# Token sums by columns, and a 31-tap convolution with an early shift, two taps on VectorE and another weight order

## The reference, cut to what matters

```python
def conv_module(h, ...):                       # first layer of the first block, for x and for ctx
    u = h @ w_pw1 + b_pw1                      # 1024 -> 2048
    a, gt = jnp.split(u, 2, axis=-1)
    u = a * jax.nn.sigmoid(gt)
    u = conv_general_dilated(u, w_dw, ...) + b_dw     # depthwise, 31 taps along the tokens
    u = jax.nn.silu(layernorm(u, ln_g, ln_b))  # mean and variance over the 1024 features
    return u @ w_pw2 + b_pw2
# every layer: mod = silu(c) @ w_mod + b_mod gives scales, shifts and gates;
#   h = rmsnorm(x, g) * (1 + sc) + sh ;  x = x + gate * rmsnorm(y, g)
#   second block: x = layer_norm(ALPHA * x + y, g, b), twice in each of two layers
```

## Time and profile before

| | us |
|---|---|
| three runs | 1966.68, 1968.42, 1971.39 |
| median | 1968.42 |
| span of the profiled execution | 1969.0 |
| TensorE busy | 1889.2 |
| VectorE, ScalarE, GpSimd busy | 1201.8, 953.6, 542.5 |

### The profile page before, as it was taken

One profiled execution on the slowest core, in us unless ns is written; L12 is line 12 of the kernel. 1 busy time (PEld: TensorE's weight loads), 2 busy tenths in 40 slices (PEclk: granted clock), 3 DMA queues, 4 the chain that ended last, 5 costly groups with the idle time before them and its releaser, 6 DMA issues.

```text
span 1969.0 us, 36121 instructions
## 1 busy us (share of the span) xinstructions
PE 1889.2 (96%) x14718; PEld 1668.6 (85%) x14718; DVE 1201.8 (61%) x2440; ACT 953.6 (48%) x1709; POOL 542.5 (28%) x685
## 2 busy tenths in 40 slices
PE   6999999999998989999998999999999999999998
PEld 4855778888886857899987989999999899989997
DVE  4989763233338575655579675685648876567473
ACT  4314532232224477544456474565555556456464
POOL 1320010000001533000021222747373322374736
PEclk9999999999999999899999999999999999999999
DMA  9335442222224254655544444455554544545551
GB/s 358 128 108 206 151 150 96 97 97 97 97 97 171 86 193 175 211 182 182 183 160 175 142 136 160 165 168 172 194 182 152 174 148 133 168 150 178 187 178 59
DMA packets 84548, 307.24 MB, mean 156 GB/s; under 512 B 9376, under 2 KB 10656, under 8 KB 84128
## 3 DMA queue, kind: packets, MB, share of 16 engines
q1 hardware_dynamic: 84384, 304.94, 45.4%
HBM read 303.86 MB, written 1.05 MB: 155 GB/s over the span
## 4 chain that ended last, share of the span: by engine, by line
PE 82%; DVE 10%; ACT 5%; DMA 2%; issue 1%; SPq 0%; POOL 0%; DVEq 0%; ACTq 0%
PE pb L540 18%; PE pb L542 18%; PE pb L541 18%; PE pb L513 7%; PE pb L514 6%; PE pb L519 6%; DVE wlo L1897 2%; DMA raw<-wstream 2%; ACT whi L1237 1%; PE pb L591 1%; DVE Y L2146 1%; PE pb L765 1%; PE pb L924 1%; PE pb L1108 1%; PE pb L1121 1%
## 5 line engine op out<-in xcount | busy, mean ns | idle before, releaser
L540 PE MATMUL pb<-Hh,whi 128*128 128x256 f32 (+1 forms) x2304 | 701.8, 305 | 1.8 <-DVE SM L2480 1.6
L542 PE MATMUL pb<-Hh,wlo 128*128 128x256 f32 (+1 forms) x2304 | 694.6, 301 | 0.0
L541 PE MATMUL pb<-Hl,whi 128*128 128x256 f32 (+1 forms) x2304 | 694.6, 301 | 0.0
L1237 ACT ACTIVATE whi<-raw 128x1024 fp32r<-128x1024 f32 x468 | 489.3, 1054 | 318.1 <-PE pb L542 171.2
L2855 POOL TENSOR_TENSOR wlo<-raw,whi 128x256 fp32r<-128x256 f32 x576 | 434.9, 790 | 734.9 <-ACT whi L1237 733.9
L1897 DVE TENSOR_TENSOR wlo<-raw,whi 128x1024 fp32r<-128x1024 f32 x324 | 421.2, 1305 | 344.1 <-ACT whi L1237 343.7
L540 PEld LDWEIGHTS pb<-Hh,whi 128*128 128x128 f32 x2304 | 441.9, 192 | 22.9 <-DVE SM L2480 2.5
L541 PEld LDWEIGHTS pb<-Hl,whi 128*128 128x128 f32 x2304 | 442.2, 192 | 15.0
L542 PEld LDWEIGHTS pb<-Hh,wlo 128*128 128x128 f32 x2304 | 442.0, 192 | 15.0
L513 PE MATMUL pb<-Hh,whi 128*128 128x256 f32 (+1 forms) x528 | 161.2, 327 | 4.6 <-ACT Hh L1311 3.2
L514 PE MATMUL pb<-Hh,wlo 128*128 128x256 f32 (+1 forms) x528 | 158.8, 322 | 0.0
(11 more groups left out here) (333 smaller groups left out, 2952.6 us busy)
## 6 DMA issues: line engine op xcount, KB each, us to landing
raw<-wstream SPq DMA_DIRECT2D x572, 512.0 KB, 3.5
X<-xin SPq DMA_DIRECT2D x2, 1024.0 KB, 7.7
out<-X SPq DMA_DIRECT2D x8, 128.0 KB, 1.8
CON<-consts SPq DMA_DIRECT2D x1, 926.0 KB, 8.6
VEC<-vecs SPq DMA_DIRECT2D x1, 662.0 KB, 9.5
CON<-consts SPq DMA_DIRECT2D x1, 147.0 KB, 3.8
VEC<-vecs SPq DMA_DIRECT2D x1, 88.0 KB, 2.0
```

What stands on the lines that cost most here:

```text
L540: e.matmul(dst, hi, xh, start=k == 0, stop=False)
L541: e.matmul(dst, hi, xl, start=False, stop=False)
L542: i = e.matmul(dst, lo, xh, start=False, stop=k == kt - 1)
L1237: e.activation(whi[:, s % NPIECE, :], raw[:, p % NRAW, :], ACT.Copy).then_inc(sig("act_hi", ("hi", p)), 1)
```

## The change

- **Statistics.** `quarters` and its copies become `columns`: for each 128 tokens one matmul with the data as the stationary operand (128 x 128) and one column of 1/1024 as the moving one. The result is one column for each 128 tokens, so a statistic is 128 x 4 (or 128 x 2). The small steps work on these, `widen` spreads a column with the identity as the moving operand (two matmuls instead of four for 256 tokens), and the constant `quad` is gone.
- **Shift.** The rough mean is summed before the first tap and spread after tap 3 (before: after taps 8 and 13); it is stored negative. The start of the taps waits for each tile of `U` in its turn.
- **Taps.** TensorE makes 29 taps. VectorE makes the last two of tiles 4 to 7 with the shift added, into four tiles `part` (`part_taps`), and 16 matmuls with `blocks` add these in; the 32nd "tap" is gone.
- **Moving out.** VectorE moves out results 4, 6 and 5, ScalarE 7; VectorE squares 5.
- **Stream.** The first four tiles of `w_pw2` stand ahead of C; C has three groups (12 pieces) and N three. Six halves of C run at taps 2, 5, 8, 11, 14 and 17, one of N at tap 26.
- **Split.** GpSimd makes no `wlo` for `w_pw1` any more; it makes those of the third and fourth piece of `w_pw2`, behind the last chunk of `DG`. VectorE makes the others.

```diff
-MODS = {"S0": (0, 2, 2), "S1": (1, 2, 2), "C": (4, 4, 1), "N": (8, 2, 1), "F": (10, 3, 1), "A": (13, 3, 1),
+MODS = {"S0": (0, 2, 2), "S1": (1, 2, 2), "C": (4, 3, 1), "N": (7, 3, 1), "F": (10, 3, 1), "A": (13, 3, 1),
...
-    mod("C")
-    run([("conv_w_pw2", (0,), m * 128) for m in range(8)], FIRST, then=["N"])
+    run([("conv_w_pw2", (0,), m * 128) for m in range(8)], FIRST, then=["C", "N"])
...
-            if tag == "pw1":
-                return s > 5 and s % 3 == 0
+            if s in (tile_turn["pw1", 15] + 3, tile_turn["pw1", 15] + 4):
+                return True
...
+            def columns(b, o, tile, n, start, stop, point):
+                for c in range(n // 128):
+                    i = e.matmul(b[:, o + c:o + c + 1], tile[:, c * 128:(c + 1) * 128], con("mean", 0, 1),
+                                 start=start and c == 0, stop=stop and c == n // 128 - 1)
+                i.then_inc(sig("pe_stat", point), 1)
...
-                for c in range(4):
-                    i = e.matmul(b[:, c * n // 4:(c + 1) * n // 4], con("quad", c, c + 1).broadcast_to((128, 128)), r,
+                for c in range(n // 128):
+                    i = e.matmul(b[:, c * 128:(c + 1) * 128], r[:, c:c + 1].broadcast_to((128, 128)), con("ident"),
                                  start=True, stop=True)
...
+            bank("norm", ("stat", "cs"), ("root", "cs"))
+            w.wait_ge(*on("cv", 0))
+            token_sums("cs", Y[:, 0:512], 512, True, False, ("zsum", "cs"))
+            w.wait_ge(*on("cv", 1))
+            token_sums("cs", Y[:, 512:1024], 512, False, True, ("sums", "cs"))
             w.wait_ge(*on("pad"))
-            for ct in range(4):
-                w.wait_ge(*on("u", 4 + ct))
-            for i_ in range(CONVW + 1):
+            for i_ in range(CONV_PE):
                 c, q = i_ // CHUNK, i_ % CHUNK
                 w.wait_ge(*on("dg", c))
                 dg = DG[:, c % 3, :, :, :]
                 for ct in range(4):
+                    if i_ == 0:
+                        w.wait_ge(*on("u", 4 + ct))
...
+                if i_ == 24:
+                    feed("N")
-                if i_ % 3 == 2 and i_ < 30:
+                if i_ % 3 == 2 and (i_ < 18 or i_ == 26):
                     bite(1)
+                if i_ == 23:
+                    mod_tr("mods")
-                if i_ == 13:
+                if i_ == 3:
                     w.wait_ge(*on("root", "cs"))
                     widen("cs", 512, ("shift",), ring="norm")
...
+            for ct in range(4):
+                w.wait_ge(*on("part", ct))
+                for r in range(4):
+                    rows = slice(32 * r, 32 * r + 32)
+                    i = e.matmul(got[r][32 * ct:32 * ct + 32, :], con("blocks", p0=32 * r, p1=32 * r + 32),
+                                 slots.at(("part", ct))[rows, :], start=False, stop=True)
...
+            def part_taps(ct):
+                t = buf(1.02, "part", ("part", ct), ("conv", 3))
+                w.wait_ge(*on("shift"))
+                w.wait_ge(*on("u", 4 + ct))
+                for i in range(CONV_PE, CONVW):
+                    if i > CONV_PE:
+                        w.wait_ge(*on("tap", 4 + ct, i - 1))
+                    points = [("tap", 4 + ct, i)] + ([("part", ct)] if i == CONVW - 1 else [])
+                    e.scalar_tensor_tensor(out=two(t), in0=U[:, 4 + ct, :, i:i + T], scalar=vec("conv_w_dw", i * 8 + 4 + ct),
+                                           in1=two(slots.at("shift") if i == CONV_PE else t), op0=ALU.mult, op1=ALU.add).then_inc(
+                        sig("dve_conv", *points), 1)
...
             shift(2)
             shift(3)
-            lo_to(("pw1", 15), 2)
+            for ct in range(4):
+                part_taps(ct)
             mod_add("C")
...
             for c, (i0, n) in enumerate(CHUNKS):
-                if c == 3:
-                    lo_to(("pw1", 15), 0)
                 for u in slots.take(0, "dg", ("dg", c), ("dgused", c)):
                     w.wait_ge(*u)
...
+            lo_to(("pw1", 15), 4)
```

More of the change, by code:

```diff
@@ L26 @@
 CONVW = 31
+CONV_PE = 29
 PAD = 15
@@ L29 @@
 CHUNK = 8
-CHUNKS = [(i, min(CHUNK, CONVW - i)) for i in range(0, CONVW, CHUNK)]
+CHUNKS = [(i, min(CHUNK, CONV_PE - i)) for i in range(0, CONV_PE, CHUNK)]
 FFN0 = [8, 7, 7]
@@ L642, in sums3 @@
                 b = slots.at(("stat", S))
-                for key, o in ((S + "b", 128), (S + "c", 256)):
+                for key, o in ((S + "b", 4), (S + "c", 8)):
                     w.wait_ge(*on("acc", key))
[L645 to L648, removed]
+                    columns(b, o, slots.at(("acc", key)), 512, False, False, ("asum", key))
                 for k in (6, 7):
                     step()
-                    for key, o in ((S, 0), (S + "b", 128), (S + "c", 256)):
+                    for key, o in ((S, 0), (S + "b", 4), (S + "c", 8)):
                         w.wait_ge(*on("sq", key, k))
[L653 to L657, removed]
+                        columns(b, o, slots.at(("sq", key, k)), 512, False, o == 8 and k == 7,
+                                ("sums", key) if k == 7 else ("xsum", key, k))
                 step()
@@ L666, in sums_y @@
                 tile = slots.at(("acc", S) if k is None else ("sq", S, k))
[L667 to L670, removed]
+                columns(b, 0, tile, 512, not k, False, ("asum", S) if k is None else ("xsum", S, k))
             def acc_sums(S, n, until=None):
@@ L747, in norm_sums @@
                 w.wait_ge(*on("fin", k))
-                quarters("cz", Y[:, k * 512:(k + 1) * 512], 512, first, last, ("zsum", k))
+                token_sums("cz", Y[:, k * 512:(k + 1) * 512], 512, first, last, ("zsum", k))
                 w.wait_ge(*on("sq", "cv", k))
-                quarters("cv", slots.at(("sq", "cv", k)), 512, first, last, ("sums", "cv") if last else ("xsum", "cv", k))
+                token_sums("cv", slots.at(("sq", "cv", k)), 512, first, last, ("sums", "cv") if last else ("xsum", "cv", k))
@@ L766, in tensor @@
-                if i_ == CONVW:
-                    i.then_inc(sig("pe_conv", ("dgused", c), *[("conv", r) for r in range(4)]), 1)
-                elif q == CHUNK - 1:
+                        i = e.matmul(two(got[r][32 * ct:32 * ct + 32, :]), dg[rows, ct, q, :], U[rows, 4 + ct, :, i_:i_ + T],
+                                     start=i_ == 0, stop=False)
+                if i_ == CONV_PE - 1 or q == CHUNK - 1:
                     i.then_inc(sig("pe_conv", ("dgused", c)), 1)
-                if i_ % 3 == 2 and i_ < 30:
+                if i_ == 24:
+                    feed("N")
@@ L1180, in squares @@
                             w.wait_ge(*on("csq", l, F, m))
[L1181 to L1187, removed]
+                            columns(b, 0, t, T, first and m == 4, last and m == 7, ("csum", l, F, m))
                     lin_first(keys[:4], kt, src, T, xh, xo)
```

118 lines of the change are left out of this document (53 added, 65 removed).

## The result

The changed kernel takes **2044.3 us** (median of five, 2041.6 to 2050.3) against 1968.4 (1966.7 to 1973.8): ratio 1.0376, 95% interval 1.0357 to 1.0395. Forecast were 1995.7 and a range of 1985 to 2023. The direction was right, and the time lies 49 us above the forecast and outside the range. The profiled execution of the changed kernel is the fastest of the five (2041.6 us). Its span is 2039.0 us, 70.0 more than that of before (the medians are 75.9 apart), at a mean granted clock of 0.971 instead of 0.991.

A forecast was written before the change was run, and what follows sets the result against it. TensorE was taken as the bound, busy 96% of the span. The convolution stage's 18.3 us plus 9.0 for statistics elsewhere made 27.3 on the profiled 1969.0; with the median 0.6 lower, the forecast was 1995.7 us, range 1985 to 2023.

The forecast's parts named there:

- The stand: Inside the convolution's taps, TensorE waits from 135.4 for a load held up by GpSimd, until 151.1: 15.6 us.
- first norm: Statistics of the kernel's first norm, in the new column form: +0.5 us.
- The likeliest case: At VectorE's shift subtraction GpSimd comes in, then alternates with taps; forecast 1995.7 us, chance 0.40.
- (a): Rival: GpSimd comes in at the next boundary of VectorE's taps, at 134.8; 1991.2 us, chance 0.25.
- (b): Rival: GpSimd stays locked out while taps follow without a gap, until 163; stall 39 us, 2019.4 us, chance 0.23.
- The price of a column sum: On TensorE, a 512-token sum costs 0.88 us in a string, 0.81 in a stream; bounds 0.81 and 0.95.
- the slow clock: Behind TensorE's stop inside the convolution, 6 us at half speed: 3.0 us.
- statistics 22.2: All sums in column form: 9.0 us outside the convolution and 13.2 for the twenty sums around it.
- the norms behind `w_pw2` and behind the FFN: Dearer sums less shorter steps: +4.1 us behind `w_pw2`, +4.9 behind the first FFN.
- The stage of the convolution: Taps, stall and the sums behind them: the stage shifts later by 18.3 us (18.2+0.1).
- (c): Rival: no stall inside the taps, since something else frees the buffer; the sums remain; 1978.6 us, chance 0.04.
- (d): Rival: column sums cost what quarters cost, weight loads hidden beneath other matmuls; -6.4 us, 1962, chance 0.05.

The follow-up runs named there:

- run 1: Changed kernel with all sums and spreads back in the old form of four quarters, all else as changed: 1986.7 us, ratio 1.0071.
- run 2: Kernel before the change with only its sums and spreads in the column form, nothing else changed: 2033.2 us, ratio 1.0307.
- early_lo: Changed kernel with GpSimd's two low halves of `w_pw2` made ahead of the fourth chunk of `DG` instead of behind it: 2028.4 us, ratio 1.0286.
- wide32: Changed kernel with each column sum moving 32 columns (the mean and 31 of zeros) instead of one: 2023.7 us, ratio 1.0259.
- quarters_early: Changed kernel with sums and spreads in quarters and GpSimd's two low halves ahead of the fourth chunk of `DG`: 1973.2 us, ratio 1.0012.
- pe30: As quarters_early, with one tap moved from VectorE back to TensorE (30 taps on TensorE): 1969.6 us, ratio 0.9988.
- break_tt: As run 1, with one useless VectorE addition of two 128 x 8 operands put among its taps: 1981.9 us.
- break_ts: As break_tt, but the small 128 x 8 instruction among VectorE's taps has one operand (`tensor_scalar`): 1983.6 us, one execution.

## Why the prediction was right and wrong

**The stand: right, step by step.** The first norm made everything 5.9 us later; less that, TensorE stands from 135.4 (forecast 135.4), GpSimd's first product is done at 140.2 (139.8), the chunk at 142.8 (143.0), the low half at 147.3 (147.6), the load at 150.6 (151.1), and the stand is 15.3 us (15.6). The likeliest case was chosen for the right reason, GpSimd coming in at the shift subtraction; rivals (a) and (b) fell, (b) because a subtraction is no tap. The Trainium skill, "SBUF — State Buffer", section "Who interferes with whom", has the port pair held for one instruction; in eleven kernels here, the one before among them, a GpSimd instruction that waited stayed out while VectorE began and ended six to nine further taps, and took 5.7 to 7.8 us, and the measurement decides. TensorE's taps began at 122.2 on this scale (forecast 122.2), and the small steps from square root to second reciprocal took 2.1 us (285.48 to 287.57; forecast 2.1). That the new order of the stream removes the load wait behind the convolution held as well.

**The price of a column sum: the step that failed.** The prediction took 0.88 in a string and 0.81 in a stream, with bounds of 0.81 and 0.95, "8% either way", from single groups of eight instructions among full-size matmuls. As long as the clock is 1.00 that price is right: 0.88 to 0.92 in a string and 0.81 in a stream (660.39 to 661.20 in the changed kernel). But the rows show the shape alone, never a string of it, and nearly all of the new sums stand in strings. There the clock falls, and a sum costs 1.71 to 1.74. The bounds of 8% were bounds for the shape at full clock; they left out that a string of this shape lowers the clock of the engine that runs it. The prediction did have the slow clock, but only behind a stop. The Trainium skill, "TensorE: Matmul & The Clock Gate", section "What's actually happening", says that the clock is set by how busy the array has been recently; the four windows above are busy from end to end by the profile's own column and at 0.50, so that column isn't what the clock follows.

The terms, with what they measured: statistics 22.2 forecast in all, 58 (run 1) and 61 (run 2) measured. In the parts of the table, the norms behind `w_pw2` and behind the FFN took 11.1 us each, 22.2 together where 9.0 were forecast; the same two with 32 columns took 3.1 and 4.9. The stage of the convolution took 34.0 instead of 18.3. Of these 15.7 us, 2 are the other point at which the table is cut. Two taps and a half of `w_mod` at the low clock behind the first four sums are 3.4 (half of 186.0 to 192.9), half of the 20.5 us from 199.7 on are 10.3, and 0.5 are those four sums. The low clock behind the stand cost 2.8 (half of 156.6 to 162.1) instead of 3.0. First norm 5.9 instead of 0.5: its two sums took 3.5 us, and the halves around them 1.9 each.

```profile
18.56 1.94 PE L593 MATMUL pb<-raw,csz 128*32 128x512 f32 x8 [0.62 <-DMA raw<-wstream]
20.43 3.57 PE L632 MATMUL pb<-CON,tmpb 128*128 128x1 f32 x16
23.93 1.93 PE L593 MATMUL pb<-raw,csz 128*32 128x512 f32 x8
```

The low clock also took back the gain of the shorter steps: `widen`, at half speed, ends later than they do. From the square root at 285.48 to the first use at 289.94 there are 4.5 us, against 4.3 in the earlier trace rows.

**As a check on the sum:** 118 us at half speed less the 35 of before cost 41.5 us. The stand was at the low clock for some 11 us in which nothing ran, which costs nothing (-5.8), and 3.0 were forecast: 32.7. The first norm's low clock lies before the first clock record (32.4 us; the windows before it show 1.00 while the halves take 1.9 us) and isn't in the mean: +5.4. That makes 38 of the 43 us by which the spans miss the forecast. I can't place the last 5. Behind the first FFN the parts of the table are 8.4 above the forecast, but short stretches at 0.50 count in these too, and single runs differ by as much.

**The rivals (c) and (d)** fell: there was a stall, and the sums weren't cheap. No rival had the sums dearer than forecast, so the range ended at 2023. The chance that the prediction left for "what I don't see" was 0.03, and this is where the time fell.

## What to carry over

- A rewrite that makes few columns move past large stationary data must be priced as a string, at either level of the clock: a busy TensorE isn't yet a fast one. Moving 31 columns of zeros along kept the clock at 1.00 in the strings of nine here at next to no cost, though not in the one of twelve; quarters stayed cheaper still.
- If a buffer's release hangs on GpSimd while VectorE works through a long run of two-input instructions such as these taps, ask what is queued in front of the releasing instruction and at which instruction of VectorE it got in before. Here moving two low halves ahead of a chunk of products was worth 16 us, and 13.5 with the sums in quarters.
- Work taken off the engine that bounds a stage is worth no more than the room on the engine that takes it.

## What the runs showed of the hardware

- The granted clock was 0.50 with TensorE busy 100%, in 17.0 us of strings of sums that move one column (271.4 to 288.4), and 1.00 in the same norm when they move 32 (256.8 to 268.1 in `wide32`), at the same 0.9 us a sum at full clock.
- GpSimd waiting at VectorE's taps: one 128 x 8 instruction of another kind (0.43 us, with one operand or two) let exactly one of its instructions in; one of 128 x 400 (0.57 us, one run) started an alternation that held for all eleven instructions behind it.
- Not explained: in `early_lo` a low half asked for at 120.30, in the middle of taps, came in at VectorE's next boundary (its first instruction took 1.25 us); `quarters_early` (117.68) and `pe30` (119.00) show the same. GpSimd had last run 1.2 us before; the ones that were kept out had rested for 14 us or more, except the second products of `break_tt` and `break_ts`. Whether it is the rest or the moment within a tap, no run here tells.
